# Gate sums broadcast by DMA through DRAM in place of matrix products, with the scratch fill issued earlier

## The chip, the core and the metric

The kernel runs on one core of one Trainium2 chip. The metric is device time in microseconds (us) of one execution of the whole program, median of several runs. A core has TensorE (PE, with its weight loads listed as PEld), VectorE (DVE), ScalarE (ACT), GpSimd (POOL) and SyncE (SP); here SP issues every DMA.

## What is computed

Two transformer layers over 256 tokens of width 1024, in fp32. Two places use running sums of a gate, and the change touches only how these sums reach the 128 partitions.

The first layer has "forgetting" attention (8 heads of 64) beside a banded attention, then cross-attention to a memory, then a feed-forward block:

```python
logf = jax.nn.log_sigmoid(f_logit)            # (B, S, 8)
c = jnp.cumsum(logf, axis=1)                  # over all 256 tokens
logits = q.k * scale + c[t] - c[s]            # c[t] is constant in a row: softmax drops it
p = softmax(where(t >= s, logits, -inf))
```

The second layer has a gated delta rule (8 heads of 128) beside sparse attention, then a feed-forward block. The kernel works the delta rule in two chunks of 128 tokens:

```python
g = -exp(a_log) * softplus(g_a + dt_bias)     # (B, S, 8)
g_cum = cumsum(g)                             # inside a chunk
decay[i, j] = exp(g_cum[i] - g_cum[j])        # for i >= j, per head and chunk
a_mat = strict_lower((k * beta) @ k.T * decay)
qk    = lower(q @ k.T * decay)
```

## The kernel before

**Weights.** All weights stream through four raw slots of 1 MB (`w_raw`, 128x2048 fp32) in 'units' of 1 MB, in a fixed order: fq, fk, fv, cq, ck, cv, mk, mv, out, mq, mo, ff1, ff2, then akv, iq, aq, qkv/z, ga, gb, out2, up, down. For each unit ACT makes a rounded high part (`unit_hi`, L401), DVE the remainder (`unit_lo`, L407), and PE multiplies high x high, high x low and low x high (L457 to L459 and L469 to L471). `advance_hi(u)` and `advance_lo(u)` split the unit two ahead of `u`. The high part of unit u may be made when PE has finished unit u-3, its load may be issued when PE has finished unit u-4.

**Queues.** Each engine runs one list of instructions in program order and waits on semaphores. The order is written by hand: `between` and `gate_tick` functions interleave attention items, transposes and splits with the unit products. SP's list is a loop over units (L2010 to L2032); before the load of certain units it issues another DMA, and any wait in it holds back all that follows.

**First gate sum.** At L2323 DVE scans the transposed log-gates to `cum` (8 heads on 8 partitions x 256), negates them into `sel_r` (L2325), POOL multiplies them with a selector into `sel_l` (L2049; `sel_l` is the first 104 partitions of `foxb`), and PE multiplies by ones: four products 8x512 in `fb_pe` (L863), put between the four parts of unit cv[1]. DVE adds the causal mask and writes `xn[:,1]` and `foxb` (L870, L872, `fb_dve`). The attention items then read these as `bias` in L793; the first item follows.

**Second gate sum.** `gates2_dve_sum` scans into `cum` (L1288), copies and negates (L1290, L1291), POOL builds a 40x2048 selector product (`gates2_pool`, L1295). Much later, between units ga[1] and ga[2], `dt_pe` (L1664) makes g_cum[i] - g_cum[j] by four products 40x512, `dt_dve` (L1669) adds the triangular mask, four instructions of 128x512, and `dt_act` (L1676) takes the exponential, four of 128x512. The result `DT` is used by `kdec_dve` and `ap_dve` (L1699). Around it run `tok_pe/act/dve` (transposes of q, k, v to token order, L1582, L1591, L1593, L1600) and `back_pe/act` (L1648, L1655).

**Scratch.** The triangular inverse of the second layer passes 16x16 blocks through DRAM. `blocks_zero_sp` (L1740) fills one scratch, 1032 KB, with zeros; its rows are 129 elements, 516 B. It is issued before the load of ff2[0].

Of the kernel before, what the change touches and what calls it, by code (L numbers as in the profile page):

```python
# [12 lines left out]
P = 128  # L13
# [27 lines left out]
C_ID, C_CAUSAL, C_ZERO, C_SEL, C_DMASK = 0, 128, 384, 640, 648  # L41
# [14 lines left out]
def constants():  # L56
# [5 lines left out]
    for h in range(8):  # L62
        c[[h, 32 + h, 64 + h, 96 + h], C_SEL + h] = 1
# [127 lines left out]
def build_program(nc, w, consts, small, rel, out):  # L191
# [3 lines left out]
    with ctx:  # L195
# [39 lines left out]
        sel_l = foxb[0:104]  # L235
        sel_a = sb("sel_a", [104, S])
        sel_r = sb("sel_r", [104, S])
        cum = sb("cum", [8, S])
        gate8 = sb("gate8", [P, 8, 16])

        def softmax_buffers(at, tag):
# [74 lines left out]
        d2 = ExitStack()  # L317
        sb("under_DT", [P, 4 * NT * D + GH * GD + 2 * 512], at=d2)
        DT = sb("DT", [P, NT, GH, P], at=d2)
        d2.close()  # L320
# [36 lines left out]
        fb_mm, fb_done = sem("fb_mm"), sem("fb_done")  # L357
        gate_v, gate_a, gate_tr, gate_ct, sel_done = [sem(n) for n in ("gate_v", "gate_a", "gate_tr", "gate_ct", "sel_done")]
# [8 lines left out]
        g2_in, g2_a, g2_g, g2_tr, g2_ct, g2_sel, g2_tm, g2_eg = [sem("g2_" + n) for n in ("in", "a", "g", "tr", "ct", "sel", "tm", "eg")]  # L367
# [7 lines left out]
        back_mm, back_copied, dt_mm, dt_add, dt_done, kdec_done, ap_mm, ap_done = [sem(n) for n in (  # L375
            "back_mm", "back_copied", "dt_mm", "dt_add", "dt_done", "kdec_done", "ap_mm", "ap_done")]
# [481 lines left out]
        FB_BANK = (aux[0], aux[3], aux[1], aux[2])  # L858
# [7 lines left out]
        def fb_dve(dve):  # L866
            for j in range(4):
                dve.wait_ge(fb_mm, j + 1)
                b = FB_BANK[j][:].rearrange("p (h s) -> p h s", h=2)
                dve.tensor_tensor(xn[:, 1, 2 * j * P:(2 * j + 2) * P].rearrange("p (h s) -> p h s", h=2), b[:, :, 0:P],  # L870
                                  both(cst[:, C_CAUSAL + P:C_CAUSAL + 2 * P]), ALU.add)
                dve.tensor_tensor(foxb[:, 2 * j:2 * j + 2, :], b, both(cst[:, C_CAUSAL:C_CAUSAL + 2 * P]), ALU.add).then_inc(fb_done, 1)  # L872
            dve.drain()
# [409 lines left out]
        def gates2_dve_sum(dve):  # L1283

            dve.wait_ge(g2_tr, 1)
            for t in range(NT):
                ts = slice(t * P, (t + 1) * P)
                dve.tensor_tensor_scan(cum[:, ts], sel_a[0:8, ts], aux[3][0:8, ts], 0.0, ALU.mult, ALU.add)  # L1288
            dve.drain()
            dve.tensor_copy(sel_r[0:8, :], cum[:]).then_inc(g2_ct, 1)  # L1290
            dve.tensor_scalar(sel_a[32:40, :], cum[:], -1.0, None, ALU.mult).then_inc(g2_ct, 1)  # L1291

        def gates2_pool(pool):
            pool.wait_ge(g2_ct, 2)
            pool.tensor_tensor(sel_l[0:40], both(sel_a[0:40, :], 8),  # L1295
                               cst[0:40, C_SEL:C_SEL + 8].unsqueeze(2).broadcast_to([40, 8, S]), ALU.mult).then_inc(g2_sel, 1)

        def gates2_pe_tm(pe):
            pe.wait_ge(g2_ct, 2)
# [1438 lines left out]
```

## Time and profile before

| | us |
|---|---|
| runs before: median (lowest to highest of 3) | 940.32 (940.08 to 940.42) |
| the profiled execution, its own time | 943.22 |
| its span, first to last instruction | 941.4 |
| PE busy in it | 913.6 |
| DVE busy / ACT busy / POOL busy | 581.7 / 510.0 / 97.9 |
| mean granted TensorE clock | 0.996 of full speed |

The profiled execution is 1.8 us longer than its span and 2.9 us longer than the median of the runs, as it carries the profiler. In the rows below a start is counted from the span's start. Matmul records overlap: each is listed with its latency, and the rate is the distance between two starts. An entry in square brackets is the time that the engine stood idle before the row, and what released it.

### The profile page before, as it was taken

The page shows a single profiled execution, that of the slowest core. Times are in us where ns is not written, and L with a number is a line of the kernel's source. Part 1 is how long each engine was busy: PE and PEld are TensorE (multiplying, and loading weights), DVE is VectorE, ACT ScalarE, POOL GpSimd, SP SyncE. Part 2 cuts the span into 40 slices and gives each one's busy share as a digit, 9 for nine tenths or more (in the row PEclk, how much of TensorE's full clock was granted, in tenths as well). Part 3 has the DMA queues.
Part 4 walks back from the last instruction along what each step waited for, and adds up shares of the span by engine and source line. Part 5 has one row for each costly group of instructions (what it writes and reads, how often), then busy time and mean ns, then how long its engine had stood idle before and what let it go on. Part 6 is the DMA issues. An engine that isn't in the chain of part 4 may idle for free. (4 is left out here: it accounts for less than half of the span.)

```text
span 941.4 us, 14648 instructions
## 1 busy us (share of the span) xinstructions
PE 913.6 (97%) x5688; PEld 801.4 (85%) x5688; DVE 581.7 (62%) x909; ACT 510.0 (54%) x921; POOL 97.9 (10%) x115
## 2 busy tenths in 40 slices
PE   5999999999999999999999999999999999999998
PEld 5997887888899997887778989978899789998886
DVE  5457455764676636435666998889655676665343
ACT  4464666665565534334567668786255365443330
POOL 1011000000000000001010412240143101000000
PEclk9999999999999999999999999999999999999999
DMA  9754442362455595555354544352450265655552
GB/s 337 245 179 135 135 135 90 135 211 80 134 180 180 180 242 177 185 178 183 131 179 135 179 135 141 129 179 90 101 180 1 96 208 174 188 186 179 180 188 79
DMA packets 110051, 150.11 MB, mean 159 GB/s; under 512 B 6688, under 2 KB 68256, under 8 KB 109856
## 3 DMA queue, kind: packets, MB, share of 16 engines
q1 hardware_dynamic: 109984, 149.20, 49.3%
q8 instruction: 45, 0.74, 0.3%
q14 instruction: 22, 0.18, 0.1%
HBM read 145.90 MB, written 3.28 MB: 158 GB/s over the span
## 5 line engine op out<-in xcount | busy, mean ns | idle before, releaser
L407 DVE TENSOR_TENSOR s_w_lo<-s_w_raw,s_w_hi 128x2048 fp32r<-128x2048 f32 (+1 forms) x198 | 317.8, 1622 | 183.8 <-ACT s_w_hi L401 183.6
L401 ACT ACTIVATE s_w_hi<-s_w_raw 128x2048 fp32r<-128x2048 f32 (+1 forms) x198 | 262.8, 1346 | 162.2 <-PE acc L459 114.9
L469 PE MATMUL acc<-s_h_hi,s_w_hi 128*128 128x256 f32 x800 | 228.8, 286 | 0.8 <-DVE s_h_lo L693 0.8
L470 PE MATMUL acc<-s_h_lo,s_w_hi 128*128 128x256 f32 x800 | 227.0, 284 | 0.0
L471 PE MATMUL acc<-s_h_hi,s_w_lo 128*128 128x256 f32 x800 | 227.0, 284 | 0.0
L469 PEld LDWEIGHTS acc<-s_h_hi,s_w_hi 128*128 128x128 f32 x800 | 154.1, 193 | 1.6 <-issue 1.2
L470 PEld LDWEIGHTS acc<-s_h_lo,s_w_hi 128*128 128x128 f32 x800 | 154.2, 193 | 0.3
L471 PEld LDWEIGHTS acc<-s_h_hi,s_w_lo 128*128 128x128 f32 x800 | 154.0, 193 | 0.0
L457 PE MATMUL acc<-s_w_hi,s_hid_hi 128*128 128x512 f32 x224 | 89.1, 398 | 2.5 <-DVE s_w_lo L407 2.5
L459 PE MATMUL acc<-s_w_hi,s_hid_lo 128*128 128x512 f32 x224 | 89.2, 398 | 0.0
L458 PE MATMUL acc<-s_w_lo,s_hid_hi 128*128 128x512 f32 x224 | 89.1, 398 | 0.0
L457 PE MATMUL acc<-s_w_hi,s_h_hi 128*128 128x512 f32 x176 | 72.0, 409 | 0.4 <-DVE s_w_lo L407 0.4
L459 PE MATMUL acc<-s_w_hi,s_h_lo 128*128 128x512 f32 x176 | 69.4, 394 | 0.0
L458 PE MATMUL acc<-s_w_lo,s_h_hi 128*128 128x512 f32 x176 | 69.2, 393 | 0.0
L1073 ACT ACTIVATE s_hid_r<-acc 128x512 f32<-128x512 f32 x32 | 19.2, 600 | 64.0 <-PE acc L471 56.5
L457 PEld LDWEIGHTS acc<-s_w_hi,s_hid_hi 128*128 128x128 f32 x224 | 42.4, 189 | 13.0 <-issue 2.7
L459 PEld LDWEIGHTS acc<-s_w_hi,s_hid_lo 128*128 128x128 f32 x224 | 42.3, 189 | 10.4
L458 PEld LDWEIGHTS acc<-s_w_lo,s_hid_hi 128*128 128x128 f32 x224 | 42.4, 189 | 10.3
L457 PEld LDWEIGHTS acc<-s_w_hi,s_h_hi 128*128 128x128 f32 x176 | 33.4, 190 | 13.0 <-issue 5.1
L497 PE MATMUL acc<-s_w_hi,s_h_hi 128*128 128x512 f32 x96 | 38.6, 402 | 2.4 <-DVE s_h_lo L718 2.3
L459 PEld LDWEIGHTS acc<-s_w_hi,s_h_lo 128*128 128x128 f32 x176 | 33.4, 190 | 7.4
L1506 POOL TENSOR_TENSOR s_qkvT<-s_qkvT,s_cprod 128x255 f32<-128x255 f32 (+2 forms) x36 | 29.4, 817 | 96.6 <-ACT s_cprod L1495 93.2
(328 smaller groups left out, 1449.2 us busy)
## 6 DMA issues: line engine op xcount, KB each, us to landing
s_w_raw<-in_w_in SPq DMA_DIRECT2D x44, 1024.0 KB, 5.2
s_w_raw<-in_w_ff SPq DMA_DIRECT2D x32, 1024.0 KB, 5.2
s_w_raw<-in_w_mlp_up SPq DMA_DIRECT2D x16, 1024.0 KB, 5.4
s_w_raw<-in_w_mlp_down SPq DMA_DIRECT2D x16, 1024.0 KB, 5.0
s_w_raw<-in_w_out SPq DMA_DIRECT2D x8, 1024.0 KB, 5.3
s_w_raw<-in_w_mk SPq DMA_DIRECT2D x4, 1024.0 KB, 4.9
s_w_raw<-in_w_mv SPq DMA_DIRECT2D x4, 1024.0 KB, 5.0
s_w_raw<-in_w_mq SPq DMA_DIRECT2D x4, 1024.0 KB, 5.0
```

The lines of the kernel that those rows point to most:

```text
L401: act.activation(w_hi[u % SPLIT_SLOTS][:, cs], w_raw[u % RAW_SLOTS][:, cs], ACT.Copy).then_inc(w_hi_done, 4 if q is None else 1)
L407: dve.tensor_tensor(w_lo[u % RAW_SLOTS][:, cs], w_raw[u % RAW_SLOTS][:, cs], w_hi[u % SPLIT_SLOTS][:, cs].bitcast(F32), ALU.subtract).then ...
L457: pe.matmul(o, hi[:, k, ts], wh[:, cs], start=q["first"] and kk == 0, stop=False)
L458: pe.matmul(o, hi[:, k, ts], wl[:, cs], start=False, stop=False)
L459: i = pe.matmul(o, lo[:, k, ts], wh[:, cs], start=False, stop=q["last"] and kk == 3)
L469: pe.matmul(o, wh[:, cs], hi[:, k, :], start=k == 0, stop=False)
L470: pe.matmul(o, wh[:, cs], lo[:, k, :], start=False, stop=False)
L471: i = pe.matmul(o, wl[:, cs], hi[:, k, :], start=False, stop=k == KC - 1)
L497: pe.matmul(o, hi[:, k, ts], wh[:, cs], start=r["first"] and kk == 0, stop=False)
L1073: act.activation(hid_r[:, j % 2, :], hid_bank(tag, j)[:], ACT.Relu).then_inc(relu_done, 1)
L1506: i = pool.tensor_tensor(qkvT[:, c, d:S], qkvT[:, c, d:S], cprod[:, j % 2, tap, 0:S - d], ALU.add)
```

## The change

The four products of the first sum and the four of the second go, and with them the selectors and POOL's two instructions. Each sum is written by DMA from `cum` to a DRAM buffer of 8 KB, and read back by a second DMA with a zero stride over partitions, which writes all of `foxb` (128x2048, 1 MB). `DT` now lives in `foxb` and is worked on in place. The sign moves into the DVE operations; the c[i] part of the decay becomes a per-partition bias of the exponential, so the exponential is split by head: 16 instructions of 128x128 in place of 4 of 128x512. The mask of the second sum becomes two DVE instructions of 128x1024, one inside the sparse attention and one behind the third `tok_dve`. SP issues the first pair of DMAs before the load of mk[1], and the second pair before the two loads that come four and five units behind aq[1]. The zero fill of the scratch moves from before ff2[0] to before ff1[0], still the first layer.

```diff
-        def fb_pe(pe, between):
+        def row_out_sp(sp, k):
+            if k:
+                sp.wait_ge(g2_ct, NT)
+                sp.dma_start(row_dram[1].rearrange("n h s -> h n s"), cum[:].rearrange("h (n s) -> h n s", n=NT)).then_inc(row_out[1], 16)
+            else:
+                sp.wait_ge(gate_ct, 1)
+                sp.dma_start(row_dram[0], cum[:]).then_inc(row_out[0], 16)
+        def row_in_sp(sp, k):
+            flat = row_dram[1].rearrange("(o n) h s -> o (n h s)", o=1) if k else row_dram[0].rearrange("(o h) s -> o (h s)", o=1)
+            sp.wait_ge(row_out[k], 16)
+            sp.dma_start(foxb[:].rearrange("p h s -> p (h s)"), flat.broadcast_to([P, 8 * S])).then_inc(row_in[k], 16)
+        def fb_dve(dve):
+            dve.wait_ge(row_in[0], 16)
             for j in range(4):
-                pe.matmul(FB_BANK[j][:], sel_a[0:8, 0:P], sel_l[0:8, 2 * j:2 * j + 2, :], start=True, stop=True).then_inc(fb_mm, 1)
-                between(j)
...
+                b = foxb[:, 2 * j:2 * j + 2, :]
+                dve.tensor_tensor(xn[:, 1, 2 * j * P:(2 * j + 2) * P].rearrange("p (h s) -> p h s", h=2),
+                                  both(cst[:, C_CAUSAL + P:C_CAUSAL + 2 * P]), b[:, :, 0:P], ALU.subtract)
+            dve.drain()
             for j in range(4):
...
+                b = foxb[:, 2 * j:2 * j + 2, :]
+                dve.tensor_tensor(b, both(cst[:, C_CAUSAL:C_CAUSAL + 2 * P]), b, ALU.subtract)
             dve.drain()
...
         def gates2_dve_sum(dve):
             dve.wait_ge(g2_tr, 1)
+            dve.wait_ge(row_out[0], 16)
...
-            dve.drain()
-            dve.tensor_copy(sel_r[0:8, :], cum[:]).then_inc(g2_ct, 1)
-            dve.tensor_scalar(sel_a[32:40, :], cum[:], -1.0, None, ALU.mult).then_inc(g2_ct, 1)
-        def gates2_pool(pool):
...
         def gates2_act_eg(act):
             act.wait_ge(g2_tm, 1)
+            act.activation(gate8[:, 0, :], aux[3][:, 0:16], ACT.Copy, scale=-1.0).then_inc(g2_eg, 1)
             act.activation(gate8[:, 5, :], aux[3][:, 0:16], ACT.Exp).then_inc(g2_eg, 1)
...
-        def dt_pe(pe, b):
...
+        def dt_dve(dve, n):
+            if n == 0:
+                dve.wait_ge(row_in[1], 16)
+            dve.tensor_tensor(DT[:, n], DT[:, n], both(cst[:, C_DMASK:C_DMASK + P], GH), ALU.add).then_inc(dt_add, 1)
         def dt_act(act, b):
             n, g = b // 2, b % 2
-            act.wait_ge(dt_add, b + 1)
-            v = DT[:, n, 4 * g:4 * g + 4, :]
-            act.activation(v, v, ACT.Exp).then_inc(dt_done, 1)
+            act.wait_ge(dt_add, n + 1)
+            act.wait_ge(g2_eg, 1)
+            for h in range(4 * g, 4 * g + 4):
+                v, c = DT[:, n, h, :], GH * n + h
+                i = act.activation(v, v, ACT.Exp, bias=gate8[:, 0, c:c + 1])
+            i.then_inc(dt_done, 1)
...
-                if u == of["ff2"][0]:
+                if u == of["ff1"][0]:
                     blocks_zero_sp(sp)
+                if u == of["mk"][1]:
+                    row_out_sp(sp, 0)
+                    row_in_sp(sp, 0)
+                if u == of["aq"][1] + RAW_SLOTS:
+                    row_out_sp(sp, 1)
+                if u == of["aq"][1] + RAW_SLOTS + 1:
+                    row_in_sp(sp, 1)
...
-            for b in range(3):
+            for b in range(2):
                 tok_act(act, b)
+            for b in range(2):
+                dt_act(act, b)
+            tok_act(act, 2)
             advance_hi(act, of["qkv"][10])
             qkv_act_tanh(act, 9)
-            for b in range(3, 6):
+            for b in range(3, 5):
                 tok_act(act, b)
+            for b in range(2, 4):
+                dt_act(act, b)
+            tok_act(act, 5)
             advance_hi(act, of["qkv"][11])
...
-            for b in range(4):
-                dt_act(act, b)
...
+                if i == len(DSA) // 2 - 1:
+                    dt_dve(dve, 0)
             attention_dve(dve, DSA, I_DSA, between)
...
             for b in range(3):
                 tok_dve(dve, b)
+            dt_dve(dve, 1)
...
-            fb_pe(pe, lambda j: mm("cv", 1, parts=[j]))
+            mm("cv", 1)
...
-            pe.wait_ge(fb_done, 2)
             attention_pe(pe, FOX, 0, between)
...
-            mm("ga", 0, 1)
-            for b in range(4):
-                dt_pe(pe, b)
-            mm("ga", 2)
+            mm("ga", 0, 1, 2)
```

## Rows read from the trace of the kernel before

**Rows 1.** The page, busy time: us, share of the span, instructions.
```profile
PE 913.6 (97%) x5688; PEld 801.4 (85%) x5688; DVE 581.7 (62%) x909; ACT 510.0 (54%) x921; POOL 97.9 (10%) x115
```

**Rows 2.** Timeline of PE, 82 to 97: start, us, engine, line, operands, idle before.
```profile
82.29 0.39 PE L458 MATMUL acc<-s_w_lo,s_h_hi 128*128 128x512 f32 x1
82.51 0.39 PE L459 MATMUL acc<-s_w_hi,s_h_lo 128*128 128x512 f32 x1
82.83 1.12 PE L863 MATMUL aux<-s_foxb,s_sel_a 8*128 8x512 f32 x2
...
93.37 0.49 PE L778 MATMUL aux<-s_mqT 64*128 64x128 f32 x4
...
96.81 0.44 PE L812 MATMUL aux<-s_cst,s_P 128*128 128x128 f32 x2 [0.91 <-ACT s_P L801]
```

**Rows 3.** Timeline of DVE around the first gate sum.
```profile
69.96 0.68 DVE L2323 TENSOR_TENSOR_SCAN s_cum<-s_sel_a,aux 8x256 f32<-8x256 f32 x1 [1.11 <-PE aux L2553]
...
87.25 0.42 DVE L870 TENSOR_TENSOR s_xn<-aux,s_cst 128x256 f32<-128x256 f32 x1
87.58 0.68 DVE L872 TENSOR_TENSOR s_foxb<-aux,s_cst 128x512 f32<-128x512 f32 x1
...
93.89 0.29 DVE L793 CUSTOM_DVE_ANT_0 s_L<-aux,s_xn 128x128 f32<-128x128 f32 x1 [0.97 <-PE aux L778]
```

**Rows 4.** Timeline of ACT, its start and the same stretch.
```profile
0.72 1.28 ACT L605 ACT_TABLE_LOAD   x1 [0.72 <-PEq L2726]
4.31 0.63 ACT L605 ACTIVATE s_junk<-s_x 128x512 f32<-128x512 f32 x1 [2.31 <-DMA s_x<-in_x]
...
83.02 1.91 ACT L401 ACTIVATE s_w_hi<-s_w_raw 128x2048 fp32r<-128x2048 f32 x1 [1.38 <-PE acc L459]
94.58 1.28 ACT L801 ACT_TABLE_LOAD   x1
95.87 0.40 ACT L801 ACTIVATE s_P<-s_L,s_nmax 128x128 f32<-128x128 f32 x1
```

**Rows 5.** The page, DMA issues: count, KB each, us from issue to landing.
```profile
s_w_raw<-in_w_mk SPq DMA_DIRECT2D x4, 1024.0 KB, 4.9
...
blk_u_dram<-s_cst SPq DMA_DIRECT2D x1, 1032.0 KB, 17.1
```

**Rows 6.** Timeline of SP's queue: the issues next to the moved and added DMAs.
```profile
75.70 0.37 SPq L2032 DMA_DIRECT2D s_w_raw<-in_w_mk  x1
...
217.77 0.37 SPq L2032 DMA_DIRECT2D s_w_raw<-in_w_mo  x1
243.40 3.09 SPq L2032 DMA_DIRECT2D s_w_raw<-in_w_ff  x2
...
330.24 0.60 SPq L1740 DMA_DIRECT2D blk_u_dram<-s_cst  x1
```

**Rows 7.** Timeline of ACT behind the zero fill.
```profile
349.44 1.91 ACT L401 ACTIVATE s_w_hi<-s_w_raw 128x2048 fp32r<-128x2048 f32 x1 [8.91 <-DMA s_w_raw<-in_w_ff]
```

**Rows 8.** Timeline of PE, first product of ff2.
```profile
353.89 0.47 PE L457 MATMUL acc<-s_w_hi,s_hid_hi 128*128 128x512 f32 x1 [2.48 <-DVE s_w_lo L407]
```

**Rows 9.** Windows: length, busy PE, PEld, DVE, ACT, POOL, granted clock, DMA share, GB/s.
```profile
354.00:360.00 6.00, 6.00 (x20) 4.75 (x21) 5.69 (x7) 3.47 (x6) 0.00 (x0) 0.72 0.38 140
```

**Rows 10.** Timeline of DVE: idle places of the moved mask, and where it stands now.
```profile
603.65 0.69 DVE L820 COPY s_PT<-aux 128x512 f32<-128x512 f32 x1 [2.17 <-PE aux L812]
...
616.04 2.29 DVE L407 TENSOR_TENSOR s_w_lo<-s_w_raw,s_w_hi 128x2048 fp32r<-128x2048 f32 x1 [1.67 <-ACT s_w_hi L401]
...
637.78 2.48 DVE L1669 TENSOR_TENSOR s_DT<-s_cst,aux 128x512 f32<-128x512 f32 x4
```

**Rows 11.** Timeline of PE, the third back-transposes.
```profile
657.56 2.42 PE L1648 MATMUL aux<-s_cst,s_qh 128*128 128x128 f32 x16 [1.65 <-DVE s_APT L1699]
```

**Rows 12.** One line by its source: ns min/median/max, first and last start us.
```profile
L1452 ACT ACTIVATE s_aqk<-s_aqk,s_hrms x4: 386/389/403, 535.8 to 536.7; 128x128 f32<-128x128 f32 x4
```

**Rows 13.** Timeline of ACT among the token transposes.
```profile
619.63 0.60 ACT L1591 ACTIVATE s_kdec<-aux 128x512 f32<-128x512 f32 x1 [1.22 <-DVE s_hsum L1600]
```

More of the change, by code:

```diff
@@ L38 @@
 AHEAD = SPLIT_SLOTS - 1
-C_ID, C_CAUSAL, C_ZERO, C_SEL, C_DMASK = 0, 128, 384, 640, 648
+C_ID, C_CAUSAL, C_ZERO, C_DMASK = 0, 128, 384, 640
 C_LEVEL = C_DMASK + P
@@ L61, in constants @@
     c[:, C_CAUSAL + P:C_CAUSAL + 2 * P] = np.where(f > r, NEG, 0)
-    for h in range(8):
-        c[[h, 32 + h, 64 + h, 96 + h], C_SEL + h] = 1
     c[:, C_DMASK:C_DMASK + P] = np.where(f >= r, 0, NEG)
@@ L356, in build_program @@
         set_done, rel_done = sem("set_done"), sem("rel_done")
-        fb_mm, fb_done = sem("fb_mm"), sem("fb_done")
-        gate_v, gate_a, gate_tr, gate_ct, sel_done = [sem(n) for n in ("gate_v", "gate_a", "gate_tr", "gate_ct", "sel_done")]
+        row_out, row_in = [[sem(f"row_{what}{k}") for k in range(2)] for what in ("out", "in")]
+        gate_v, gate_a, gate_tr, gate_ct = [sem(n) for n in ("gate_v", "gate_a", "gate_tr", "gate_ct")]
         sc_done, l_done, p_done, pt_done, ptc_done, pv_done, rinv_done, y_done = [sem(n) for n in (
@@ L365, in build_program @@
         stored = sem("stored")
-        g2_in, g2_a, g2_g, g2_tr, g2_ct, g2_sel, g2_tm, g2_eg = [sem("g2_" + n) for n in ("in", "a", "g", "tr", "ct", "sel", "tm", "eg")]
+        g2_in, g2_a, g2_g, g2_tr, g2_ct, g2_tm, g2_eg = [sem("g2_" + n) for n in ("in", "a", "g", "tr", "ct", "tm", "eg")]
         set2_done, ik_done, rope_i, iqT_mm, iqT_copied = [sem(n) for n in (
@@ L374, in build_program @@
             "gate_tanh", "tok_mm", "tok_copied", "tok_sq", "tok_ss", "tok_rms", "tok_done")]
-        back_mm, back_copied, dt_mm, dt_add, dt_done, kdec_done, ap_mm, ap_done = [sem(n) for n in (
-            "back_mm", "back_copied", "dt_mm", "dt_add", "dt_done", "kdec_done", "ap_mm", "ap_done")]
+        back_mm, back_copied, dt_add, dt_done, kdec_done, ap_mm, ap_done = [sem(n) for n in (
+            "back_mm", "back_copied", "dt_add", "dt_done", "kdec_done", "ap_mm", "ap_done")]
         blk_zero, blk_out, blk_in, blk_done, blk_back, a_done, pa_done, pa_mm = [sem(n) for n in (
@@ L1621, in tok_scale_dve @@
                 dve.wait_ge(tok_copied, 8)
-                dve.wait_ge(g2_eg, 1)
+                dve.wait_ge(g2_eg, 2)
             if k < 2:
@@ L1655, in back_act @@
             act.activation(dst, aux[b % 4][:].rearrange("p (h s) -> p h s", h=4), ACT.Copy).then_inc(back_copied, 1)
-        def dt_pe(pe, b):
-            n, g = b // 2, b % 2
-            pe.wait_ge(tok_copied, b + 5)
-            if b == 0:
-                pe.wait_ge(g2_sel, 1)
-            ts = slice(n * P, (n + 1) * P)
-            pe.matmul(aux[b][:], sel_r[0:40, ts], sel_l[0:40, 4 * g:4 * g + 4, ts], start=True, stop=True).then_inc(dt_mm, 1)
-        def dt_dve(dve, b):
-            n, g = b // 2, b % 2
-            dve.wait_ge(dt_mm, b + 1)
-            dve.tensor_tensor(DT[:, n, 4 * g:4 * g + 4, :], both(cst[:, C_DMASK:C_DMASK + P], 4),
-                              aux[b][:].rearrange("p (h s) -> p h s", h=4), ALU.subtract).then_inc(dt_add, 1)
+        def dt_dve(dve, n):
+            if n == 0:
+                dve.wait_ge(row_in[1], 16)
+            dve.tensor_tensor(DT[:, n], DT[:, n], both(cst[:, C_DMASK:C_DMASK + P], GH), ALU.add).then_inc(dt_add, 1)
         def dt_act(act, b):
             n, g = b // 2, b % 2
-            act.wait_ge(dt_add, b + 1)
-            v = DT[:, n, 4 * g:4 * g + 4, :]
-            act.activation(v, v, ACT.Exp).then_inc(dt_done, 1)
+            act.wait_ge(dt_add, n + 1)
[4 more added lines that the diff above has]
+            i.then_inc(dt_done, 1)
         def kdec_dve(dve):
@@ L2653, in _ @@
                     mm("qkv", 11)
-            mm("ga", 0, 1)
-            for b in range(4):
-                dt_pe(pe, b)
-            mm("ga", 2)
+            mm("ga", 0, 1, 2)
             for b in range(8, 12):
```

43 lines of the change are left out of this document (9 added, 34 removed).

## The prediction

> **What bounds the kernel now.** First the page: PE is busy in 97% of the span, so a removed PE instruction shortens the run wherever nothing else ends last at that place, and what matters of the other engines is where PE waits for them [rows 1]. Then I read the timelines of PE, DVE and ACT at the three places that the change touches, asking at each what would be last without the removed work.
>
> At the first sum PE is the last. Its last matmul of cv[0] starts at 82.51, 0.22 behind the one before; four products (1.12 long each) lie among the 24 matmuls of cv[1], and the first scores follow at 93.37 [rows 2]. DVE makes the masks behind its split of mk[1] and then waits for the products; it starts the first item's mask at 93.89 [rows 3]. PE then waits 0.91 for ACT's exponential, and makes the first transposes at 96.81 [rows 2, 4].
>
> At the zero fill a DMA is the last. 1032 KB in pieces of 516 B take 17.1 us, where 1 MB of weights takes 4.9 [rows 5]. It is issued at 330.24 [rows 6], so it lands at about 347.3; ACT stands idle for 8.91 us until 349.44, waiting for a feed-forward weight load [rows 7], and PE then waits 2.48 us at 353.89 for the remainder [rows 8]. The granted clock of the 6 us behind that idle is 0.72: part of it ran at the lower of the two levels, half of full speed [rows 9].
>
> At the second sum DVE is the last: its mask of 2.48 us [rows 10] stands in the same list as what PE waits for, 1.65 us, at 657.56 [rows 11].
>
> **The change part by part.**
>
> *First sum, what goes.* Without the products the 24 matmuls end 24 x 0.22 to 0.23 us behind 82.51; with a small gap the first scores start at about 88.2 in place of 93.37: 5.1 us less on PE [rows 2]. That is all there is to win here.
>
> *First sum, what is late next.* DVE's chain is now SBUF only, but it still begins behind the split of mk[1], at 87.25. It has the same eight instructions at 0.33 and about 0.60 us (0.68 less the overlap with the next, as 87.25 and 87.58 show) [rows 3]: 4 x 0.33 + 4 x 0.60 = 3.7, plus two drains, about 0.1 each: first item's mask at 91.1. The page of before has these instructions reading PSUM; I take the same price for SBUF. The scores are there by then. Two masks start 0.2 apart, and the exponential can start at 91.5. The table load of 1.28 us [rows 4] must not stand behind that wait. At the kernel's start such a load runs from 0.72 to 2.00, and the idle of 2.31 that waits for data comes behind it [rows 4]: loads go ahead of the wait of their instruction. So it runs at about 89.5 to 90.8, behind the two copies out of the accumulators, and is hidden. From exponential to transposes is 96.81 - 95.87 = 0.94 [rows 2, 4]: transposes at 92.5 or 92.6. **Gain 4.2.** If the table load isn't hidden, 1.28 less: 2.9. If the masks were free, PE's 5.1. PE has some 2.5 us of products between first scores and transposes (93.37 to 96.81 less 0.91), so it would idle 1.9 us at about 90.7 in place of 0.91.
>
> *First sum, the DMAs.* The scan ends at 69.96 + 0.68 = 70.6 [rows 3]. The write of 8 KB isn't in the trace; it lies between nothing and a 1 MB load's 4.9 [rows 5], so it is there by 75.5. SP waits for it, and behind SP stands the load of mk[1], now issued at 75.70 [rows 6], so it hardly moves. The read writes 1 MB; the nearest row is the weight load, 4.9, the far one the fill, 17.1. I take 4.9, since it writes rows of 8 KB into SBUF as the weight load does, where the fill is 516 B pieces: it lands by 80.4, long before 87.25. The mk[1] load shares the DMA engines with it and lands by 85.3 at the latest, if the two come one behind the other. ACT wants it at 83.02 [rows 4], DVE two us later. I take nothing for this, and up to 2.3 as a bound.
>
> *Zero fill.* It goes ahead of ff1[0], and so right behind the mo[3] load issued at 217.77; the next issue, the ff1 loads, is at 243.40 [rows 6]. That leaves 25.6 us of quiet for 17.1, and its source is a constant: free. If it still met the mo[3] load, that is wanted only some 25 us later. At the old place ACT's wait of 8.91 goes, PE's 2.48 with it [rows 7, 8], and the low stretch: 0.28 of 6 us is 1.7 [rows 9]. **Gain 4.1**, bounds 2.4 (the clock falls elsewhere) and 4.2. What is late next there is PE itself.
> The Trainium skill, "TensorE: Matmul & The Clock Gate", section "HAM oscillation — how this bites in real kernels", says that a wait of PE can throttle it, so that the next tile starts cold. The trace agrees: the 0.72 stands right behind the 2.48 of idle. By this rule the new 1.9 us at 90.7 could cost what the old wait cost, which is rival A.
>
> *Second sum, PE.* Four products of 512 columns go; at most the 1.12 us of their like, 4.5 in all [rows 2]. PE isn't what ends last here, so most of this becomes idle at the wait of 657.56.
>
> *Second sum, DVE.* The 2.48 of mask leaves the busy stretch before 657.56, and comes back as two instructions of about 1.24 each. One falls into the idle of 2.17 before 603.65; the other behind the third token step, into the 1.67 before 616.04 [rows 10]. Both fit: nothing is paid for them. If they didn't, they would give 2.48 back, and the gain would be zero.
>
> *Second sum, ACT.* Each exponential is now 128x128 with a bias of its own per partition. Such instructions stand 0.30 us apart [rows 12], so the 16 take 4.8, in two groups of eight of 2.4 each. The first group falls into a wait of ACT for DVE like the one before 619.63. The second meets only that one, 1.22 [rows 13]: ACT comes 2.4 - 1.2 = 1.2 us late to the split behind it, and DVE and PE follow it. **Net gain 2.48 - 1.2 = 1.3**, bounds 0 (ACT's delay is larger by a further group) and 2.5 (no delay). The Trainium skill, "ScalarE: Activation LUTs", section "What ACT_TABLE_LOAD costs", gives an ACTIVATE with a bias from memory 280 ns and 0.833 ns per element, with 93 ns overlap; that would be 0.29 each, and the trace agrees.
>
> *Gates of the second layer.* ACT gets one more instruction, 128x16, less than the 0.30 of a 128-column one [rows 12], where PE waits for ACT: 0.2 lost, bounds 0 and 0.3. The scans keep their length; POOL's two selector products and DVE's copies were waited for by nobody but the removed matmuls, so they give 0. The second pair of DMAs is issued about 100 us before DVE wants it, behind loads that SP holds for PE anyway: 0, and if the write were late, the load behind it would still have four slots of slack.
>
> **Sum:** 4.2 + 4.1 + 1.3 - 0.2 = 9.4. The profiled execution was 943.2, so its changed counterpart should be 933.8. It stands 2.9 above the median of the runs, 940.3; I take the same distance: **930.9**.
>
> **The rivals.**
>
> A. *The clock falls at the new idle.* PE would wait 1.9 us at 90.7, and the stretch behind would run partly at the lower level, as after 353.89: 1.7 lost [rows 9], 932.6. For it: the place follows waits of 0.91 [rows 2]. Against it: 1.9 is nearer to the waits of 0.91 and 1.65 [rows 2, 11] than to 2.48, and with a mean clock of 0.996 in the whole run few waits can have cost it. Chance 0.12.
>
> B. *The fill isn't what stalls ff.* Then the 8.91 of ACT stays, caused by other loads in the queue, and only 5.3 is won: 935.0. Against it: 330.24 + 17.1 = 347.3 is close to 349.44 [rows 5 to 7]. Chance 0.06.
>
> C. *The second sum gives nothing, or all of DVE's share.* 932.2 if ACT's delay passes on in full and adds a group, 929.7 if PE's freed time covers it. These lie around the forecast and are part of its own range.
>
> D. *PE is the bound all the way.* Then its work counts in full: 5.1 + 4.1 + 4.5 - 0.2 = 13.5, giving 926.8. Against it: the DVE chain of 3.7 us behind 87.25 is there in any case. It would need masks at less than a third of the price. Chance 0.08.
>
> E. *The first table load is not hidden, or mk[1] is late.* 2.9 or 1.9 in place of 4.2: 932.2 to 933.2. Chance 0.15.
>
> F. *The broadcast read is slow; slower than before.* All 128 destinations read the same 8 KB. If that goes at the fill's pace, it lands at 75.5 + 17.1 = 92.6, and mk[1] behind or beside it at 92.6 to 97.5, say 95.0. DVE's split starts 2.0 behind the landing (83.02 to 85.0), takes 2.2, then 3.9 of masks and 1.4 to the transposes: 95.0 + 9.6 = 104.6, 7.8 later than 96.81. With 4.1 + 1.3 - 0.2 = 5.2 won elsewhere the run is 2.6 slower: 942.9. It decides from a landing of mk[1] at 96.8 + 5.2 - 9.6 = 92.4 on. Against it: the read moves large rows, and small pieces are what marks out the fill. Chance 0.04, and 0.03 for a read in between, whose loss about equals the gain.
>
> **How the numbers follow.** The forecast holds 0.52 with C, then A 0.12, B 0.06, D 0.08, E 0.15, F 0.07. The forecast's own range is 929.5 to 932.5. The range for 8 in 10 takes in A, E and B at the top, 935.0, and at the bottom half the way to D, since the bounds of single terms (4.2 to 5.1, 1.3 to 2.5) reach 928.8 together: **927.5 to 935.0**. What it leaves out is F and most of D. About 0.2%, 1.9 us, is what a measurement of this kernel can tell from no change: faster 0.93, same 0.04, slower 0.03, where same and slower come from F and from B together with losses at the first sum.
>
> **What would show it.** In the changed profile the first transposes of the attention start 4.2 us earlier than 96.81, DVE's first mask starts at 91, and the table load ends before it. The read lands before 80.4, and no engine waits for it. ACT has no long wait for a feed-forward weight near 340, PE none before ff2, and the clock there is full. Before the third back-transposes PE's wait is longer than 1.65 by 2 to 3 us, since its products have gone and DVE has gained less. Wrong would be: a wait of DVE for the read, a wait of ACT for mk[1] above 2.3 us, a clock of 0.7 behind the first items, or the old stall back under another load.

## The result and the profile after

The changed kernel takes 930.14 us, median of 4 runs (928.95 to 931.53), beside 940.37 before (940.08 to 941.06): ratio 0.9883, 95% interval 0.987 to 0.9896. That is 10.2 us less than before (9.8 to 12.2 by the interval), where 9.4 was forecast. Its profiled execution took 928.95 us, the lowest of the four. PE is busy 17.3 us less than in [rows 1]:

```profile
PE 896.3 (97%) x5672; PEld 795.1 (86%) x5672; DVE 574.6 (62%) x903; ACT 511.9 (55%) x934; POOL 90.7 (10%) x113
```

Lines of the helpers stand 7 lower than before (L401 is now L394, L459 is L452). SP at the first sum, to hold against [rows 6]; columns as in the rows of before:

```profile
69.27 0.37 SPq L2031 DMA_DIRECT2D s_w_raw<-in_w_mk  x1
70.20 0.35 SPq L861 DMA_DIRECT2D cum_dram<-s_cum  x1
74.86 0.35 SPq L867 DMA_DIRECT2D s_foxb<-cum_dram  x1
75.25 0.43 SPq L2031 DMA_DIRECT2D s_w_raw<-in_w_mk  x1
```

The write is waited for from 70.20 to 74.86, 4.7 us for 8 KB, while the 1 MB load issued at 69.27 is still under way (its like takes 5.1 us here); the load of mk[1] is issued at 75.25. The DMA issues of two stretches, 60 to 95 us and then 190 to 240 us (KB each, us from issue to landing), give the read and the fill, to hold against [rows 5]:

```profile
s_foxb<-cum_dram SPq DMA_DIRECT2D x1, 1024.0 KB, 4.8
```
```profile
blk_u_dram<-s_cst SPq DMA_DIRECT2D x1, 1032.0 KB, 12.8
```

DVE, ACT and PE at the first sum, to hold against [rows 2 to 4]:

```profile
69.50 0.68 DVE L2320 TENSOR_TENSOR_SCAN s_cum<-s_ones,aux 8x256 f32<-8x256 f32 x1 [1.12 <-PE aux L2549]
...
86.91 1.43 DVE L873 TENSOR_TENSOR s_xn<-s_cst,s_foxb 128x256 f32<-128x256 f32 x4
88.41 2.50 DVE L878 TENSOR_TENSOR s_foxb<-s_cst,s_foxb 128x512 f32<-128x512 f32 x4
91.03 0.29 DVE L786 CUSTOM_DVE_ANT_0 s_L<-aux,s_xn 128x128 f32<-128x128 f32 x1
```
```profile
82.68 1.92 ACT L394 ACTIVATE s_w_hi<-s_w_raw 128x2048 fp32r<-128x2048 f32 x1 [1.51 <-DMA s_w_raw<-in_w_mk]
...
89.00 1.28 ACT L794 ACT_TABLE_LOAD   x1
91.37 0.40 ACT L794 ACTIVATE s_P<-s_L,s_nmax 128x128 f32<-128x128 f32 x1 [1.08 <-DVE s_nmax L786]
```
```profile
91.39 0.69 PE L771 MATMUL aux<-s_mqT 64*128 64x128 f32 x4 [1.53 <-DVE s_nmax L786]
92.30 0.44 PE L805 MATMUL aux<-s_cst,s_P 128*128 128x128 f32 x2 [0.22 <-ACT s_P L794]
```

DVE's masks stand without a gap from 86.91 and the first item's mask follows at 91.03 (91.1 forecast). The table load is done at 90.28, and ACT then waits 1.08 for DVE, so it is hidden. First transposes: 92.30 in place of 96.81. The whole profiled execution was 0.45 us ahead by then (the scan at 69.50, not 69.96), so 4.1 is won here. mk[1] lands just before 82.68, and ACT's wait there is 1.51 in place of 1.38: 0.1 us late, no more. One thing went faster unseen: DVE's split that ran beside POOL's selector product took 4.98 us before and takes 2.29 now (71.84 and 71.38 in the two traces), but ACT came last behind it and hid the gain.

ACT and PE at the second sum, to hold against [rows 11, 13]:

```profile
607.04 2.46 ACT L1667 ACTIVATE s_foxb<-s_foxb,s_gate 128x128 f32<-128x128 f32 x8
...
610.33 1.95 ACT L394 ACTIVATE s_w_hi<-s_w_raw 128x2048 fp32r<-128x2048 f32 x1
```
```profile
614.74 0.50 PE L450 MATMUL acc<-s_w_hi,s_h_hi 128*128 128x512 f32 x1 [1.06 <-DVE s_w_lo L400]
...
645.04 1.23 PE L1646 MATMUL aux<-s_cst,s_qh 128*128 128x128 f32 x8 [2.98 <-DVE s_APT L1691]
```

The second group of exponentials takes 2.46, ACT's split behind it is late, and PE waits 1.06 for it. Before the third back-transposes PE's wait has grown from 1.65 to 2.98, by 1.3 us, where 2 to 3 us more were forecast.

So far every place looks nearly as forecast. But the two profiled executions differ by 943.22 - 928.95 = 14.3 us, the medians by 10.2, and the forecast sum was 9.4. Matching the matmuls of both traces one by one (how much earlier each starts in the changed one) shows where it came from: 0.5 before the first sum, 4.1 at it, 4.3 at the fill and the half clock behind it, 1.3 at the second sum, minus 0.2 in small losses (0.1 of it at the gates), and **4 us in stretches that the change doesn't touch**: 0.8 in the 40 us behind the first sum, 1.5 in ff2 and 1.7 in down; the small rest lies scattered. PE is never idle in these stretches and the granted clock is 1.00 in both. Only the instructions differ, by 1 to 7 ns each. One group of products of ff2 (362 to 442 us; count, busy us, mean ns):

```profile
L457 PE MATMUL acc<-s_w_hi,s_hid_hi 128*128 128x512 f32 x103 | 40.7, 395 | 0.0
```
```profile
L450 PE MATMUL acc<-s_w_hi,s_hid_hi 128*128 128x512 f32 x88 | 34.1, 388 | 0.0
```

The first of these rows is of the kernel before, the second of the changed one; the counts differ only because the window holds more of ff2 before. From one start to the next the matmuls are 0.2333 and 0.2289 us apart. The 384 matmuls of down show it, first and last, before and then after: 383 steps in 89.37 us, and in 87.66.

```profile
848.08 0.39 PE L457 MATMUL acc<-s_w_hi,s_hid_hi 128*128 128x512 f32 x1
...
937.45 0.40 PE L499 MATMUL acc<-s_w_hi,s_hid_lo 128*128 128x512 f32 x1
```
```profile
835.71 0.39 PE L450 MATMUL acc<-s_w_hi,s_hid_hi 128*128 128x512 f32 x1
...
923.37 0.40 PE L492 MATMUL acc<-s_w_hi,s_hid_lo 128*128 128x512 f32 x1
```

The experiments had two questions: where does this come from, and what is each part worth?

### The profile page after: what moved, and what is told of

Read it like the earlier page. It is cut to its first block and busy times, and to the rows that moved or that the text cites. A ratio compares the mean times of both kernels' runs of the same rounds, so it can differ in the third digit from the quotient of the medians.

```text
span 927.0 us, 14627 instructions
## 1 busy us (share of the span) xinstructions
PE 896.3 (97%) x5672; PEld 795.1 (86%) x5672; DVE 574.6 (62%) x903; ACT 511.9 (55%) x934; POOL 90.7 (10%) x113
## 5 line engine op out<-in xcount | busy, mean ns | idle before, releaser
L400 DVE TENSOR_TENSOR s_w_lo<-s_w_raw,s_w_hi 128x2048 fp32r<-128x2048 f32 (+1 forms) x198 | 312.4, 1595 | 174.9 <-ACT s_w_hi L394 174.6
L394 ACT ACTIVATE s_w_hi<-s_w_raw 128x2048 fp32r<-128x2048 f32 (+1 forms) x198 | 262.8, 1346 | 152.7 <-PE acc L452 101.9
L452 PE MATMUL acc<-s_w_hi,s_hid_lo 128*128 128x512 f32 x224 | 88.3, 394 | 0.0
L450 PE MATMUL acc<-s_w_hi,s_hid_hi 128*128 128x512 f32 x224 | 86.9, 388 | 0.0
L452 PE MATMUL acc<-s_w_hi,s_h_lo 128*128 128x512 f32 x176 | 68.7, 391 | 0.0
L452 PEld LDWEIGHTS acc<-s_w_hi,s_hid_lo 128*128 128x128 f32 x224 | 42.1, 188 | 8.4
L452 PEld LDWEIGHTS acc<-s_w_hi,s_h_lo 128*128 128x128 f32 x176 | 33.0, 188 | 7.2
```

The lines of the kernel that those rows point to most:

```text
L394: act.activation(w_hi[u % SPLIT_SLOTS][:, cs], w_raw[u % RAW_SLOTS][:, cs], ACT.Copy).then_inc(w_hi_done, 4 if q is None else 1)
L400: dve.tensor_tensor(w_lo[u % RAW_SLOTS][:, cs], w_raw[u % RAW_SLOTS][:, cs], w_hi[u % SPLIT_SLOTS][:, cs].bitcast(F32), ALU.subtract).then ...
L450: pe.matmul(o, hi[:, k, ts], wh[:, cs], start=q["first"] and kk == 0, stop=False)
L452: i = pe.matmul(o, lo[:, k, ts], wh[:, cs], start=False, stop=q["last"] and kk == 3)
```

## The experiments

Each was compared with runs of the kernel before on the same chip. Those had medians of 940.69 (e1 to e4), 940.47 (e5 to e8) and 942.69 (e9, e11, e12, e13). The changed kernel was not run again, so a difference from its 930.14 crosses two sets, and is good to 1 us at best. In the last set the kernel before took 940.52 to 944.54 in eight runs, and 5095.38 in a ninth. Its three runs at a mean clock of 0.998 took 940.52 to 941.34, as in the other sets, and the five at 0.994 to 0.996 took 942.66 and more. So the ratios of the last four flatter them by about 2 us, and the plain times are the better guide.

**e1: the fill alone, moved.**

```diff
-                if u == of["ff2"][0]:
+                if u == of["ff1"][0]:
                     blocks_zero_sp(sp)
```

> The kernel before with one edit: the zero fill is issued ahead of the first ff1 load in place of the first ff2 load. My theory: the fill held back one feed-forward weight load, and it ends 4.1 us earlier (2.5 of PE's wait and 1.7 of the half clock behind it), so the ratio is 0.9956, and ACT has no long wait near 340 us. Rival (the stall comes from other loads in the queue): no change, ratio 1.000, and ACT still waits about 9 us for a feed-forward weight. All addresses in SBUF are those of the kernel before, so its profile also tells whether the matmuls of ff2 and down stand 0.233 us apart (the profiled execution of the kernel before) because of the addresses, or only in that one execution: by addresses 0.233, by the execution any value, most likely 0.229.

939.25 us, ratio 0.999 (0.9977 to 1.0003): 1.4 us less than before by the medians (by the interval anything from none to 2.2), not 4.1. ACT's long wait is gone, so the cause is right and the size isn't. The matmuls of ff2 stand 0.2333 apart here, so that distance belongs to the kernel and not to one execution.

**e2: the first sum alone.** The kernel before with the first sum's two DMAs, masks from SBUF, and neither products nor selector:

```diff
-            pe.wait_ge(sel_done, 1)
-            fb_pe(pe, lambda j: mm("cv", 1, parts=[j]))
+            mm("cv", 1)
...
+                if u == of["mk"][1]:
+                    row_out_sp(sp, 0)
+                    row_in_sp(sp, 0)
```

> The kernel before with the first gate sum alone sent through DRAM: two DMAs ahead of the mk[1] load, no products at cv[1], no selector on POOL, DVE masks from SBUF. The second sum and the fill stay as before. My theory (DVE ends last): the first transposes of the attention start 4.2 us earlier, the run is 4.2 us shorter, ratio 0.9955. Rival (PE is the bound all the way): 5.1 us, ratio 0.9946. Rival (the read or the late mk[1] load costs): under 3 us, ratio above 0.997.

936.75 us, ratio 0.9958 (0.9946 to 0.997): 3.9 us less, near the 4.2 forecast, and not 5.1. Here the fill is at its old place, and PE waits for it too, but less than in [rows 8]:

```profile
349.66 0.47 PE L457 MATMUL acc<-s_w_hi,s_hid_hi 128*128 128x512 f32 x1 [1.68 <-DVE s_w_lo L407]
```

**e3: the fill put back into the changed kernel.** The first edit, reversed.

> The changed kernel with the fill put back ahead of the first ff2 load. My theory: what the fill costs doesn't depend on the sums, so this is 4.1 us slower than the changed kernel: about 934.3 us, 6 us faster than before, ratio 0.9935, with ACT's wait of 9 us and PE's of 2.5 us back. Rival (the fill only met that load because of where the kernel before stood): no stall, about 930.1, ratio 0.989.

930.76 us, ratio 0.9899 (0.9885 to 0.9914): 0.6 us more than the changed kernel by the times and 1.5 by the ratios, which can't be told from nothing, and in any case not 4.1. By position in the two traces the fill's place costs 1.1. ACT's wait is back with 7.30 us, and PE's with 0.88:

```profile
346.78 0.48 PE L450 MATMUL acc<-s_w_hi,s_hid_hi 128*128 128x512 f32 x1 [0.88 <-DVE s_w_lo L400]
```

PE's wait at this one place, with the fill where it was, is 2.48, 1.68 and 0.88 in three traces (2.19 in e8 and 0.88 in e5 below), and the half clock followed only behind 2.48 and 2.19. ACT's wait for the load is 8.91, 8.11, 7.30, 8.61 and 7.31 in the same traces, 6.4 more than PE's each time: PE pays for just what the load is late. The five traces are of five kernels, one execution each, so how much of the spread lies between executions of one kernel is not shown. The profile of before is the dearest of them.

**e4: 1 KB put back.**

```diff
         ones8 = sb("ones8", [8, S])
+        sb("pad", [P, S])
```

> The changed kernel with 1 KB per partition of unused space behind the ones, so that everything allocated behind it (the hidden activations among it) stands at the address of the kernel before. The profiles of before and after differ by 3.1 us in ff2 and down, where nothing was changed: their matmuls stand 0.2333 us apart before and 0.2287 after, both at full clock. Theory addresses: here they stand 0.2333 apart and the run is 3 us slower than the changed kernel, about 933.2, ratio 0.9924. Theory execution (one execution is a little slower than another): the distance has nothing to do with the addresses, the run takes about 930.1, ratio 0.989.

929.7 us, ratio 0.9886 (0.9873 to 0.9899); the matmuls stay 0.2289 apart. Neither theory had it: by e1 it isn't the execution, and 1 KB isn't the shift that matters. The 1 KB did not restore the old address either, as the expectation has it, but one 32 B off. What was left was that difference: without `C_SEL` the constants are 8 columns narrower, and all that is allocated behind them moves by 32 B more.

**e5 and e6: 32 B alone, and 32 B undone.** The same edit in the kernel before and in the changed one:

```diff
         cst = sb("cst", [P, N_CONST])
+        sb("gap", [P, 8])
```

> The kernel before with one edit: 8 unused columns (32 B per partition) behind the constants. In all three kernels built on the one before, the ff2 and down matmuls stand 0.2333 us apart; in all three built on the changed one 0.2289, also where 1 KB was padded back. What still differs is that the changed kernel's constants are 8 columns (32 B) narrower, so that all buffers behind them, the hidden activations and the rounded memory among them, start at a multiple of 64 B, and before at 32 B beyond one. Theory alignment: here the matmuls stand 0.2289 apart with nothing else changed, 3.1 us less in ff2 and down and 0.8 in the first attention, ratio 0.9958. Rival (something else in the program sets that distance): 0.2333, ratio 1.000.

936.01 us, ratio 0.995 (0.9937 to 0.9962): 4.5 us less, by 32 unused bytes per partition.

> The changed kernel with the same 8 unused columns behind the constants, which puts its buffers 32 B off. Theory alignment: 0.2333 us between the matmuls of ff2 and down, 3.9 us slower than the changed kernel, about 934.0, ratio 0.993. Rival: 0.2289 and 930.1, ratio 0.989. This is also the changed kernel without the side effect of its narrower constants, so it measures the change that was costed.

934.15 us, ratio 0.9931 (0.9919 to 0.9944): 4.0 us more than the changed kernel. The products of ff2 (mean ns), of e5 and then of e6:

```profile
L458 PE MATMUL acc<-s_w_hi,s_hid_hi 128*128 128x512 f32 x97 | 37.7, 389 | 0.0
```
```profile
L451 PE MATMUL acc<-s_w_hi,s_hid_hi 128*128 128x512 f32 x90 | 35.5, 395 | 0.0
```

A shift of 32 B is shown as the cause, in both directions. All that lies behind the constants moved with it; the split weights and `h_hi` lie in front and stayed. So in ff2 and down the operand that moved is the streamed one, the hidden activations. Products that stream `h_hi` are a control: 0.227 us apart (median) in all 14 traces. In e5 the distance fell even to 0.2269, below that of the changed kernel; down of e5, 383 steps in 86.84 us:

```profile
842.12 0.40 PE L458 MATMUL acc<-s_w_hi,s_hid_hi 128*128 128x512 f32 x1
...
928.96 0.39 PE L500 MATMUL acc<-s_w_hi,s_hid_lo 128*128 128x512 f32 x1
```

**e7: the exponentials later.** The second group of eight goes on ACT from between two token steps to ahead of the last tanh of qkv.

```diff
-            for b in range(3, 5):
-                tok_act(act, b)
-            for b in range(2, 4):
-                dt_act(act, b)
-            tok_act(act, 5)
+            for b in range(3, 6):
+                tok_act(act, b)
...
             gate_tick(5)
+            for b in range(2, 4):
+                dt_act(act, b)
             qkv_act_tanh(act, 11)
```

> The changed kernel with the second group of eight exponentials moved on ACT from between the fifth and sixth token step to ahead of the last tanh of qkv, where ACT stood idle 2.31 us in the profile of after. My theory (that group makes ACT 1.1 us late, and all engines after it): PE's wait of 1.06 at the first product of ga goes, the third back-transposes come 1.1 us earlier, about 929.0, ratio 0.9876. Rival (DVE's list sets the end there whatever ACT does): no change, 930.1, ratio 0.989.

928.82 us, ratio 0.9872 (0.9857 to 0.9887): 1.3 us below the changed kernel's 930.14 (1.0 by the ratios). PE's wait of 1.06 at the first product of ga is gone, and by position 0.9 is won there. The group's price was near the 1.2 of the forecast, and it could be avoided.

**e8: the second sum alone.** The kernel before with the second sum through DRAM, the first by products, the fill and the constants as they were; the diff is the second sum's part of the change.

> The kernel before with the second gate sum alone sent through DRAM (first sum by products, fill at its old place, constants at their old width, so at the old alignment). My theory (DVE frees 2.5, ACT gives back 1.1, the gates 0.2): 1.1 to 1.3 us faster, ratio 0.9987. Rival (PE's four products count in full, with the half clock behind them): 5 us faster, ratio 0.9947. Rival (nothing is won): 1.000.

939.99 us, ratio 0.9993 (0.9984 to 1.0002): 0.5 us less, which can't be told from nothing, nor, as the interval reaches 1.5, from the 1.1 expected. Windows (length, busy PE, PEld, DVE, ACT, POOL, granted clock, DMA share, GB/s) of this kernel behind its third back-transposes, which start at 655.48 in place of 657.56, behind a wait of 2.99:

```profile
656.00:660.00 4.00, 4.00 (x19) 3.25 (x18) 4.00 (x5) 2.39 (x4) 0.00 (x0) 0.62 0.74 222
```

This trace is 2.1 us ahead of before at the back-transposes (0.8 of them from before the second sum), and after the half clock only 0.6. But that loss doesn't last. In the kernel before PE waits twice more behind it:

```profile
680.29 0.50 PE L457 MATMUL acc<-s_w_hi,s_h_hi 128*128 128x512 f32 x1 [0.37 <-DVE s_w_lo L407]
...
696.05 1.07 PE L1823 MATMUL aux<-s_Tm,s_Bt 128*128 128x64 f32 x8 [0.40 <-DVE s_Tm L1863]
```

In e8 both waits are gone, and the product of 696.05 starts at 694.17:

```profile
694.17 1.06 PE L1817 MATMUL aux<-s_Tm,s_Bt 128*128 128x64 f32 x8
```

So at 700 us e8 is 1.9 ahead again. The second sum is worth 1.1 in this trace, half clock and all, and 1.2 in the changed kernel's, which has no half clock here. The other eight traces with a half clock at this place get it back too: by 700 us they stand, against the kernel that each was built on, where they stood ahead of it, within 0.3 us in seven and 0.5 better in e7.

**e13: the wider gap, on the changed kernel.** `gap` with 16 columns, which puts the hidden activations at a multiple of 128 B.

> The changed kernel with 16 unused columns (64 B per partition) behind the constants. In the runs so far the distance between the ff2 and down matmuls follows where the hidden activations start: 0.2333 us at 32 B beyond a multiple of 64 (before), 0.2289 at a multiple of 64 but not of 128 (after), 0.2269 at a multiple of 128 (the kernel before with 8 unused columns). Theory (multiples of 128 are best, also on the changed kernel): 0.2269 in ff2 and down, about 670 of these matmuls, so 1.3 us there and a little in the first attention: about 928.6, ratio 0.9873. Rival (the 0.2269 belonged to something else in that kernel): 0.2289, about 930.1, ratio 0.989.

929.02 us, ratio 0.9858 (0.9842 to 0.9874); 1.1 us below the changed kernel by the times. In the trace the matmuls of ff2 and down stand 0.2267 apart: the theory holds for them. But in the first attention, where `m_hi` and `m_lo` are loaded as weights, the same shift costs (count, busy us, mean ns):

```profile
L462 PE MATMUL acc<-s_m_hi,s_w_hi 128*128 128x256 f32 x24 | 6.9, 288 | 0.0
```
```profile
L463 PE MATMUL acc<-s_m_hi,s_w_hi 128*128 128x256 f32 x24 | 7.0, 293 | 0.0
```

The first row is of the changed kernel, the second of e13, both from 96 to 108 us. By position in the two traces that loses 0.7 us up to 120 us, where ff2 and down win 1.4; the net is below what the runs can tell.

**e9: the masks of the late items later.** The four 128x512 masks go behind DVE's work of item pairs 1 to 4.

```diff
-            for j in range(4):
-                b = foxb[:, 2 * j:2 * j + 2, :]
-                dve.tensor_tensor(b, both(cst[:, C_CAUSAL:C_CAUSAL + 2 * P]), b, ALU.subtract)
...
+                if 1 <= p <= 4:
+                    fb_dve_rest(dve, p - 1)
```

> The changed kernel with the four 128x512 masks of foxb, which only the second eight heads' items read, taken from ahead of the first item and put one each behind the DVE work of item pairs 1 to 4. My theory (DVE's list sets the first transposes, and behind it ACT's table load, which ends at 90.28, is next): the first transposes come 1.1 us earlier, at about 91.2, 929.0 us, ratio 0.9877; with PE's idle there under 1 us the clock falls less often, up to another 0.8. Rival (DVE gives the 2.4 us back among the item pairs): no change, ratio 0.989.

928.6 us, ratio 0.9853 (0.9838 to 0.9869); by the times it is 1.5 us below the changed kernel. By position the first transposes come 1.1 us earlier, as expected (91.52, in an execution that was 0.3 us behind). ACT's first exponential now follows the table load at once, and PE waits once, 0.96:

```profile
89.29 1.28 ACT L794 ACT_TABLE_LOAD   x1
90.59 0.40 ACT L794 ACTIVATE s_P<-s_L,s_nmax 128x128 f32<-128x128 f32 x1
```

The table load is the next bound behind DVE, as expected.

**e12: all three.** The wider gap and both moves together.

> The changed kernel with the three edits together: 16 unused columns, the second group of exponentials later on ACT, the four masks of foxb later on DVE. They lie in different stretches, so they should add: 1.5 + 1.3 + 1.1 = 3.9 us less than the changed kernel, about 926.2, ratio 0.985. If one of them only moves a wait, less, down to 1.5.

927.03 us, ratio 0.9832 (0.9817 to 0.9847), the fastest of all; 3.1 us below the changed kernel by the times, 3.9 expected. The 0.8 that is missing is about what the weights of the first attention lose by the gap (0.7 by position), but it is also within what two sets can differ by.

**e11: the slow read.** The first sum lies in DRAM in rows of 129, so that the read goes in pieces of 512 B.

```diff
-        row_dram = [nc.dram_tensor("cum_dram", (8, S), F32, kind="Internal").ap(),
+        row_dram = [nc.dram_tensor("cum_dram", (16, P + 1), F32, kind="Internal").ap(),
...
+                src = row_dram[0][:, 0:P].unsqueeze(0).broadcast_to([P, 16, P])
+                sp.dma_start(foxb[:].rearrange("p h (n s) -> p (h n) s", n=NT), src).then_inc(row_in[k], 16)
```

> The changed kernel whose first sum lies in DRAM in rows of 129 elements, so that the broadcast read goes in pieces of 512 B, 2048 of them, like the zero fill. It tests the price of the slow read that I named as the case in which the change loses. By that case the read takes some 17 us in place of 4.8 and lands at about 92, the load of mk[1] behind it at 92 to 97, the first transposes 9.6 us behind that load, 9 to 14 us later than 92.3: 939 to 944 us, ratio 0.999 to 1.004. Rival (512 B pieces aren't what made the fill slow): it lands within 8 us and the run stays at 930 to 932.

932.2 us (930.45 to 934.92), ratio 0.9891 (0.9872 to 0.9911): 2.1 us more than the changed kernel by the times, where 9 to 14 were expected. The issues of 60 to 95 us, and ACT and PE:

```profile
s_foxb<-cum_dram SPq DMA_DIRECT2D x1, 1024.0 KB, 5.8
```
```profile
85.57 1.92 ACT L394 ACTIVATE s_w_hi<-s_w_raw 128x2048 fp32r<-128x2048 f32 x1 [2.61 <-DMA s_w_raw<-in_w_mk]
...
94.27 1.00 PE L771 MATMUL aux<-s_mqT 64*128 64x128 f32 x4 [2.62 <-DVE s_nmax L786]
```

5.8 us in place of 4.8, not 17: pieces of 512 B cost this read 1 us, and the fill's 12.5 to 17.2 (in all traces) must come mostly from something else. It writes DRAM, and at the old place it took 15.1 to 17.2, at the new one 12.5 to 13.8; what makes it slow, no run separates. Still mk[1] came later, by 1.1 us once the 1.8 is taken off by which this execution was behind from its start. PE waited 2.62 in place of 1.53, just as much longer, and the clock stayed at half for the next 7 us:

```profile
94.00:101.00 7.00, 6.73 (x32) 6.29 (x32) 2.02 (x11) 3.28 (x11) 0.00 (x0) 0.51 0.01 3
```

So the mechanism of the losing case is real, a late mk[1] goes straight to PE, but its price was out of reach. The profiled execution is the slowest of the five, with a mean clock of 0.995; the fastest, 930.45, had 1.000. So the half clock did not come each time.

## Why the prediction was right, point by point

The time was right, and its sum only in part. By the medians of the runs:

| part | forecast | measured |
|---|---|---|
| first sum | 4.2 | 3.9 (e2) |
| fill | 4.1 | 1.4 (e1), 0.6 (e3), 1.1 by position (e3) |
| second sum with the gates | 1.3 - 0.2 = 1.1 | 0.5 (e8), 1.1 by position |
| buffers moved by 32 B | not seen | 4.0 (e6), 4.5 (e5) |
| sum | 9.4 | 9.8 with e1 and e6; 10.2 measured |

Without the side effect of the narrower constants the change is worth 940.47 - 934.15 = 6.3 us (e6), where 9.4 was forecast. That 930.9 was met within 0.8 is luck: one term was 2.7 us too large, and one of 4 was missing.

- **First sum: right**, step by step. DVE's chain was priced from instructions reading PSUM and came out nearly the same from SBUF (1.43 + 2.50 = 3.9 for the eight, 3.7 forecast, and about 0.1 for each of the two drains, which no row of before had shown). The table load went ahead of its wait. The write took 4.7, near the upper bound of 4.9, the read 4.8, and mk[1] was 0.1 late. PE idled 1.53 + 0.22 us, 1.9 forecast. Taking the exponentials' start from DVE's list and not from PE was the choice that mattered: 5.1 was on offer and 3.9 came. e9 shows that the masks were what held it.
- **Fill: the mechanism right, the size wrong.** The step that failed is "at the old place PE's 2.48 goes, and the low stretch with it". I read both from one execution that was itself 2.9 us above the median, and subtracted them from the median. In four neighbours of that kernel, one execution each, the wait was 0.88 to 2.19, and the half clock followed in one. I had put the 2.9 down to the profiler; no run bears that out, as the profiled execution of the changed kernel lies 1.2 us below its median. The distance should have been a warning about the rows that looked accidental: a wait for a DMA, and a fall of the clock.
- **Second sum: right.** DVE's list did bound it, ACT gave back 1.1 and PE's products counted for nothing; by position 1.3 net at the back-transposes, and 1.2 at 700 us (1.1 in e8). The wait grew by less than the 2 to 3 us forecast, since part of PE's freed time went to new waits ahead of it: 1.06, 0.73 and 0.63 at 614.74, 621.20 and 627.52. And the 1.65 of before was itself an accident: PE had lost 1.6 us to a half clock at 634 to 640 (granted clock 0.72), hidden behind DVE. In e1 the same code had no half clock there and waited 3.08 for the same thing, with a half clock behind it, of whose cost by 700 us all but 0.3 was back. What stood in no term is this half clock behind the longer wait; it came in 9 of 13 traces and cost next to nothing, since later waits took it up. The rows taken for the exponential's price ([rows 12]) have a scale of their own per partition and not a bias; with the bias the eight took 2.46, the same 0.30 apart. PE of e1:

```profile
652.99 1.23 PE L1648 MATMUL aux<-s_cst,s_qh 128*128 128x128 f32 x8 [3.08 <-DVE s_APT L1699]
```

- **Rival A** (the clock falls at the new wait) was given 0.12 and is no yes or no. The wait before the second scores was 1.39 in both e3 and e4. First PE and the window behind it in e3, then the same in e4:

```profile
91.25 0.70 PE L771 MATMUL aux<-s_mqT 64*128 64x128 f32 x4 [1.39 <-DVE s_nmax L786]
```
```profile
92.00:96.00 4.00, 3.83 (x33) 3.59 (x33) 1.75 (x8) 2.44 (x9) 0.00 (x0) 1.00 0.06 19
```
```profile
92.48 0.70 PE L772 MATMUL aux<-s_mqT 64*128 64x128 f32 x4 [1.39 <-DVE s_nmax L787]
```
```profile
93.00:97.00 4.00, 3.78 (x20) 3.61 (x19) 1.68 (x7) 2.71 (x9) 0.00 (x0) 0.57 0.11 34
```

  The same wait, and then 1.00 in one and 0.57 in the other. It should have been a part of each time, a share of the 1.4 to 1.5 us that the half clock cost at this place in e2, e4 and e7, and not a case of its own. By the rule of the Trainium skill that I set beside it ("TensorE: Matmul & The Clock Gate", section "HAM oscillation — how this bites in real kernels") a wait can be followed by a cold tile; the traces agree that it can, and show that at this length it need not.
- **Rivals B to F**: B (the fill isn't the cause) falls, since the wait went with the fill in e1 and came back with it in e3. C (nothing or all of DVE's share at the second sum) falls by position in both traces, 1.1 and 1.2; the medians alone don't exclude nothing. D (PE the bound all the way) falls: the first sum gave 3.9 and not 5.1 (e2), the second at most 1.5 and not 4.5 (e8). E: the table load was hidden, mk[1] late by 0.1. F's price falls by e11.

## What to carry to other kernels

Before a wait of the profile is taken as a price, look at whether it is of the kind that differs from one execution to the next (a DMA that just comes too late, the clock behind it), and at how far the profiled execution stands from the median; here that turned 4.1 us into about 1. When the time comes out as forecast, check the terms one by one all the same. When a diff changes the size of any buffer, list what is allocated behind it: 32 B moved 4 us on a kernel where nearly all the time is matmul. And where several engines end near one another, freeing the one that isn't last only makes its wait longer. Whether a half clock behind such a wait costs anything depends on what comes next: at the first items it cost 1.4 us or more for good, at the third back-transposes the next waits gave it back.

## What the runs showed of the hardware that I had not expected

**Matmul speed depends on the start address of fp32 operands in SBUF.** The distance between 128x512 matmuls of ff2 and down, with the weights unmoved and the clock at 1.00: 0.2333 us where the hidden activations start 32 B beyond a multiple of 64 (before, e1, e2, e6, e8), 0.2289 at a multiple of 64 but not of 128 (after, e3, e4, e7, e9, e11), 0.2266 to 0.2269 at a multiple of 128 (e5, e12, e13). The addresses are added up from the buffers, as said at e5. As the loaded weights, a multiple of 128 was not the best: 128x256 products with `m_hi` and `m_lo` stood 0.1138 us apart at 64 beyond it (after), 0.1184 at 32 beyond a multiple of 64 (e6), and 0.1198 at a multiple of 128 (e13). Why, no run shows.

**A small DMA behind a large one waits with it.** From the issue of the 8 KB write to the next issue, which waits for it, 4.7 us went by. The 1 MB load issued 0.9 us earlier was under way for nearly all of that, and the DMA engines were over 90% busy from 71 to 73 us. What 8 KB cost by themselves no run shows, so on a quiet queue they may be cheaper.

**A VectorE instruction slows down beside GpSimd.** In the kernel before the 128x2048 remainder took 4.98 and 5.15 us where one of POOL's two selector products of 3.60 us was running, in place of 2.29. Each time it ended 2.2 us behind POOL's product, as if it had begun only then. Without these products it takes 2.29 at both places. The first, behind the scan of the first sum:

```profile
71.84 4.98 DVE L407 TENSOR_TENSOR s_w_lo<-s_w_raw,s_w_hi 128x2048 fp32r<-128x2048 f32 x1 [0.85 <-ACT s_w_hi L401]
```

**Half clock behind a short wait comes and goes.** Behind a wait of 1.3 to 1.7 us at the first items it fell in 3 of 7 traces (e2, e4, e7, not after, e3, e6, e13), behind 2.62 (e11) for 7 us. At the third back-transposes, with waits of 3.0 to 3.1, it fell in 9 of 13 (not in after, e4, e12 and e13). What decides it, no run separates; executions of one kernel differ too, as the mean clocks of 0.994 to 0.998 in the eight runs of the kernel before in the last set show.
